# Depthwise conv of a Conformer layer: VectorE's taps merged into one instruction each, eight instead of nine taps on TensorE, and a new split of the last channel tile

## The reference, cut to what matters

```python
def conformer_conv(x, w_pw1, b_pw1, w_dw, b_dw, g_n, b_n, w_pw2, b_pw2):
    h = x @ w_pw1 + b_pw1
    a, gate = jnp.split(h, 2, axis=-1)
    h = a * jax.nn.sigmoid(gate)
    h = depthwise_conv(h, w_dw, b_dw)          # 31 taps, each channel by itself
    h = jax.nn.silu(layer_norm(h, g_n, b_n))
    return h @ w_pw2 + b_pw2
```

## Time and profile before

| | us |
|---|---|
| median of 3 runs | 3003.24 |
| lowest, highest | 3001.82, 3005.05 |
| the profiled execution's own time | 3003.5 |
| its span, first to last instruction | 3001.1 |
| TensorE busy in the span | 2876.8 |
| VectorE busy | 1640.7 |
| GpSimd busy | 911.8 |
| ScalarE busy | 749.3 |

### The profile page before, as it was taken

How to read it: one execution, slowest core, us unless ns; L and a number is a source line. 1 busy time by engine, 2 the same in 40 slices (tenths; PEclk the granted TensorE clock), 3 DMA queues, 4 the chain that set the end, 5 groups by cost and what they waited for, 6 DMA issues and landing times.

```text
span 3001.1 us, 36000 instructions
## 1 busy us (share of the span) xinstructions
PE 2876.8 (96%) x14070; PEld 2347.4 (78%) x14070; DVE 1640.7 (55%) x2612; ACT 749.3 (25%) x1717; POOL 911.8 (30%) x798
## 2 busy tenths in 40 slices
PE   8999959999999999999899899899999999999995
PEld 7888848788888888888788544487888888888884
DVE  3699974744444444444730599727444444444457
ACT  3212343221111111222111466502222111111131
POOL 3354502232233233232132333323223223223323
PEclk9999979999999999999999899999999999999998
DMA  4000003111111111111221000021111111111111
GB/s 131 29 18 25 28 1 119 29 43 31 40 43 39 33 43 43 36 43 36 71 78 32 22 1 1 23 94 36 43 36 40 31 43 43 36 36 43 43 36 70
DMA packets 158644, 124.65 MB, mean 42 GB/s; under 512 B 27905, under 2 KB 135801, under 8 KB 158488
## 3 DMA queue, kind: packets, MB, share of 16 engines
q1 hardware_dynamic: 149640, 96.83, 11.3%
q10 hardware_dynamic: 8848, 25.69, 2.3%
HBM read 112.01 MB, written 10.49 MB: 41 GB/s over the span
## 4 chain that ended last, share of the span: by engine, by line
PE 86%; DVE 9%; ACT 3%; issue 1%; DMA 0%; POOL 0%; POOLq 0%; ACTq 0%; SPq 0%; DVEq 0%
PE bank L588 26%; PE bank L593 26%; PE bank L591 26%; PE bank L953 3%; PE bank L929 2%; DVE conv_acc L1293 2%; PE bank L944 1%; DVE stats L1223 1%; DVE y L1241 1%; DVE x_lo L1249 1%; ACT y L1094 1%; DVE y L1236 1%; DVE y L1451 1%; PE bank L618 1%; ACT probs L1187 1%
## 5 line engine op out<-in xcount | busy, mean ns | idle before, releaser
L588 PE MATMUL bank<-x_hi,w_hi 128*128 128x512 f32 (+1 forms) x2688 | 957.2, 356 | 3.8 <-DVE x_lo L1249 1.6
L591 PE MATMUL bank<-x_lo,w_hi 128*128 128x512 f32 (+1 forms) x2688 | 953.4, 355 | 0.0
L593 PE MATMUL bank<-x_hi,w_lo 128*128 128x512 f32 (+1 forms) x2688 | 953.3, 355 | 0.0
L514 POOL CAST w_hi<-raw_pieces 128x512 fp32r<-128x512 f32 x348 | 329.9, 948 | 1802.9 <-issue 1363.8
L588 PEld LDWEIGHTS bank<-x_hi,w_hi 128*128 128x128 f32 x2688 | 509.5, 190 | 79.0 <-POOL w_lo L518 6.3
L591 PEld LDWEIGHTS bank<-x_lo,w_hi 128*128 128x128 f32 x2688 | 509.5, 190 | 70.6
L593 PEld LDWEIGHTS bank<-x_hi,w_lo 128*128 128x128 f32 x2688 | 509.1, 189 | 70.8
L518 POOL TENSOR_TENSOR w_lo<-raw_pieces,w_hi 128x512 fp32r<-128x512 f32 x348 | 472.2, 1357 | 27.9
L1451 DVE TENSOR_TENSOR y<-y,bank 128x512 f32<-128x512 f32 x440 | 296.2, 684 | 200.5 <-PE bank L593 198.5
L1412 DVE SCALAR_TENSOR_TENSOR gate_conv<-bank,ffn_conv_table,gate_conv 128x510 f32<-128x510 f32 x132 | 86.2, 653 | 373.5 <-ACT up_conv L1125 371.5
L1293 DVE SCALAR_TENSOR_TENSOR conv_acc<-glu,conv_table,conv_acc 128x1024 f32<-128x1024 f32 (+1 forms) x310 | 257.6, 906 | 35.4 <-ACT conv_acc L1034 35.4
(11 more groups left out here) (144 smaller groups left out, 3765.5 us busy)
## 6 DMA issues: line engine op xcount, KB each, us to landing
raw_pieces<-in_ffn_w_up_dram SPq DMA_DIRECT2D x168, 256.0 KB, 2.9
raw_pieces<-in_ffn_w_down_dram SPq DMA_DIRECT2D x84, 256.0 KB, 2.6
raw_pieces<-in_conv_w_pw_dram SPq DMA_DIRECT2D x48, 256.0 KB, 2.7
y<-in_x_prompt_dram ACTq DMA_DIRECT2D x16, 512.0 KB, 6.8
residual_dram<-y ACTq DMA_DIRECT2D x10, 512.0 KB, 2.6
y<-residual_dram ACTq DMA_DIRECT2D x10, 512.0 KB, 10.7
out_dram<-y SPq DMA_DIRECT2D x10, 512.0 KB, 2.6
raw_pieces<-in_attn_w_q_dram SPq DMA_DIRECT2D x32, 128.0 KB, 2.4
```

The source lines that it names most:

```text
L514: pool.tensor_copy(WH[:, p % RING, :], raw[:, p % RAW, :]).then_inc(piece_hi, 1)
L588: mm = pe.matmul(out, left[0], right[0], start=first, stop=False)
L591: pe.matmul(out, left[0], right[1], start=False, stop=False)
L593: return pe.matmul(out, left[1], right[0], start=False, stop=last)
```

## The change

1. `PE_TAPS` goes from 9 to 8, so VectorE has 23 taps for tiles 0 to 6 instead of 22.
2. Of these, all but the last are one instruction each, over both sequences and the 15 columns between them (1295 columns). Each waits for the one before it. The last tap stays a pair.
3. For tile 7 TensorE has 26 taps instead of 22 (`MORE_TAPS` 18), VectorE 5 instead of 9. Its sums stay in three banks (7, 6, 5). ScalarE's copies of them are gone. VectorE makes its five taps apart (`last_channels`: a tensor_scalar and four chained taps, on columns of the first chunk, then on the others), and adds each chunk's bank to them, into `conv`. `last_done` counts the three additions. TensorE's and ScalarE's work on row tiles waits for `last_done` where it waited for `conv_done`.
4. Tile 7 needs 26 high and 26 low diagonals. 24 pairs are made where 22 were; the last two pairs are made behind the high part of `glu` and ahead of two of ScalarE's copies for tile 6.
5. The row tiles of `conv_normed` are stored in another order (`NORMED_AT`), since that buffer overlays `glu` and `conv_acc`.

```diff
-    PE_TAPS = 9
-    MORE_TAPS = 13
+    PE_TAPS = 8
+    MORE_TAPS = 18
...
+                    out = bank[LAST_BANK[ch] if more else 6 + u % 2]
+                    if more and ch == 2:
+                        pe.wait_ge(sig_ready, i * 6 + 6)
+                    elif not first or u >= 2:
                         pe.wait_ge(acc_ready, i * 6 + u - 1)
...
-            pe.wait_ge(conv_done, KT)
+            pe.wait_ge(last_done, 1)
             for t in range(2):
                 turn_conv(t, KT - 1).then_inc(ct_turned, 1)
             for t in range(2, TT):
                 pe.wait_ge(ct_kept, t - 1)
+                pe.wait_ge(last_done, sum(t >= e for e in TILES_TO) + 1)
...
                         act.activation(last_glu[0], glu[:, c, :], ACT.Copy).then_inc(glu_hi_ready, 1)
+                        last_diagonals(EARLY_DIAGS, LAST_TAPS).then_inc(diag_ready, 1)
                         keep_taps(0, i, first, 1, 3)
-                        keep_taps(1, i, first)
...
-                for k in range(taps):
-                    last = k == taps - 1
-                    for c0, n, a0 in ((0, S0, 0), (S0, S1, S0 + PAD)):
-                        if k > 0:
-                            dve.wait_ge(vec_step, vs.now() - (0 if last and c0 else 1))
-                        ins = dve.scalar_tensor_tensor(
-                            out=conv[:, bass.ds(i * 2 + c, 1), c0:c0 + n] if last else acc[:, c, a0:a0 + n],
-                            in0=glu[:, c, a0 + k:a0 + k + n], scalar=tap(k), in1=acc[:, c, a0:a0 + n],
-                            op0=ALU.mult, op1=ALU.add)
-                        if not last:
-                            ins.then_inc(vec_step, vs.one())
+                n = S0 + PAD + S1
+                for k in range(taps - 1):
+                    if k > 0:
+                        dve.wait_ge(vec_step, vs.now())
+                    dve.scalar_tensor_tensor(out=acc[:, c, :], in0=glu[:, c, k:k + n], scalar=tap(k),
+                                             in1=acc[:, c, :], op0=ALU.mult, op1=ALU.add
+                                             ).then_inc(vec_step, vs.one())
                     if k == 3:
                         between()
+                dve.wait_ge(vec_step, vs.now())
+                k = taps - 1
+                for c0, n, a0 in ((0, S0, 0), (S0, S1, S0 + PAD)):
+                    ins = dve.scalar_tensor_tensor(
+                        out=conv[:, bass.ds(i * 2 + c, 1), c0:c0 + n], in0=glu[:, c, a0 + k:a0 + k + n],
+                        scalar=tap(k), in1=acc[:, c, a0:a0 + n], op0=ALU.mult, op1=ALU.add)
                 ins.then_inc(conv_done, 1)
...
-            conv_taps(1, KT // 2 - 1, taps=V_TAPS - MORE_TAPS)
+            def last_channels(a0, n, chunks):
+                tap = lambda k: conv_tab[:, KT - 1, k:k + 1]
+                part = acc[:, 1, a0:a0 + n]
+                dve.tensor_scalar(part, glu[:, 1, a0:a0 + n], tap(0), chan[:, 0, KT - 1:KT], ALU.mult, ALU.add
+                                  ).then_inc(vec_step, vs.one())
+                for k in range(1, V_TAPS - MORE_TAPS):
+                    dve.wait_ge(vec_step, vs.now())
+                    dve.scalar_tensor_tensor(out=part, in0=glu[:, 1, a0 + k:a0 + k + n], scalar=tap(k), in1=part,
+                                             op0=ALU.mult, op1=ALU.add).then_inc(vec_step, vs.one())
+                dve.wait_ge(vec_step, vs.now())
+                for ch in chunks:
+                    c0, m = CHUNKS[ch]
+                    at = GLU_COL[ch] - PAD
+                    dve.wait_ge(taps_done, 3 * (KT - 1) + ch + 1)
+                    dve.tensor_tensor(conv[:, KT - 1, c0:c0 + m], acc[:, 1, at:at + m], bank[LAST_BANK[ch]][:, 0:m],
+                                      ALU.add).then_inc(last_done, 1)
+            dve.wait_ge(conv_done, KT - 2)
+            last_channels(0, HALF, [0])
+            last_channels(HALF, HALF + PAD + S1, [1, 2])
```

More of the change, by code:

```diff
@@ L222, in trunk @@
         conv_done = sem("conv_done")
+        last_done = sem("last_channels_chunk_done")
         ct_turned = sem("conv_tile_turned")
@@ L434, in trunk @@
         EARLY = 4
+        NORMED_AT = [0, 3, 4, 5, 1, 2, 6, 7, 8, 9]
         LAST_TAPS = MORE_TAPS + PE_TAPS
@@ L439, in last_diag @@
         def last_diag(j):
-            where = slice(None), j // TILES_TO[0], cols(j % TILES_TO[0])
+            if j < EARLY_DIAGS:
+                where = slice(None), j // TILES_TO[0], cols(j % TILES_TO[0])
+            else:
+                where = slice(None), j - EARLY_DIAGS, cols(TILES_TO[0])
             return XH[where], XL[where]
         LAST_ROW = KT - 2
-        assert (LAST_TAPS - 1) // TILES_TO[0] < LAST_ROW
+        EARLY_DIAGS = LAST_ROW * TILES_TO[0]
+        LAST_BANK = [7, 6, 5]
+        assert LAST_TAPS - EARLY_DIAGS <= LAST_ROW
         last_glu = [part[:].rearrange("p k t -> p (k t)")[:, LAST_ROW * XW:LAST_ROW * XW + WIDE] for part in (XH, XL)]
@@ L654, in back_tile @@
                 for k in range(KT):
-                    mm = pe.transpose(bank[4 + 2 * (t % 2) + k // 4][:, cols(k % 4)], normed[:, t, cols(k)],
+                    mm = pe.transpose(bank[4 + 2 * (t % 2) + k // 4][:, cols(k % 4)], normed[:, NORMED_AT[t], cols(k)],
                                       ident[:])
@@ L675, in conv_taps @@
                     u = 3 * c + ch
-                    if not first or u >= 2:
+                    out = bank[LAST_BANK[ch] if more else 6 + u % 2]
+                    if more and ch == 2:
+                        pe.wait_ge(sig_ready, i * 6 + 6)
+                    elif not first or u >= 2:
                         pe.wait_ge(acc_ready, i * 6 + u - 1)
@@ L680, in conv_taps @@
                         left = last_diag(more + j) if more else (diag[:, 0, j, :], diag[:, 1, j, :])
-                        mm = product(bank[6 + u % 2][:, 0:n], left, (hi[:, at:at + n], lo[:, at:at + n]),
+                        mm = product(out[:, 0:n], left, (hi[:, at:at + n], lo[:, at:at + n]),
                                      j == -more, j == PE_TAPS - 1)
@@ L1035, in keep_taps, with last_diagonals @@
                                    bias=chan[:, 0, bass.ds(i * 2 + c, 1)]).then_inc(acc_ready, 1)
-            def last_diagonals():
+            def last_diagonals(j0, j1):
                 tables = last_hi[:].bitcast(F32), last_lo[:]
                 for part, table in enumerate(tables):
-                    for j in range(LAST_TAPS):
+                    for j in range(j0, j1):
                         ins = act.activation(last_diag(j)[part], ident[:], ACT.Copy, scale=table[:, j:j + 1])
-                ins.then_inc(diag_ready, 1)
+                return ins
             def pw1_round(i, first, last=False):
@@ L1055, in pw1_round @@
                         if last and s == 3:
-                            last_diagonals()
+                            last_diagonals(0, EARLY_DIAGS)
                     if last and c == 1:
@@ L1079, in _ @@
                 act.wait_ge(ct_turned, t + 1)
+                if t == TILES_TO[0]:
+                    act.wait_ge(last_done, 3)
                 for half in range(2):
-                    ins = act.activation(normed[:, t, half * HALF:(half + 1) * HALF],
+                    ins = act.activation(normed[:, NORMED_AT[t], half * HALF:(half + 1) * HALF],
                                          bank[2 * (t % 2) + half][:], ACT.Copy)
@@ L1325, in conv_round @@
                         conv_taps(1, i - 1, lambda: glu_low(0, i))
-            vs.rounds(dve, KT // 2 - 1, conv_round, 2 * 2 * (V_TAPS - 1))
+            vs.rounds(dve, KT // 2 - 1, conv_round, 2 * (V_TAPS - 1))
             conv_round(KT // 2 - 1, False, last=True)
-            conv_taps(1, KT // 2 - 1, taps=V_TAPS - MORE_TAPS)
+            def last_channels(a0, n, chunks):
[17 more added lines that the diff above has]
+            last_channels(HALF, HALF + PAD + S1, [1, 2])
             def conv_stats(t):
@@ L1334, in conv_stats @@
                 for half in range(2):
-                    dve.bn_stats(stats[:, t % 2, half, :], normed[:, t, half * HALF:(half + 1) * HALF]
+                    dve.bn_stats(stats[:, t % 2, half, :], normed[:, NORMED_AT[t], half * HALF:(half + 1) * HALF]
                                  ).then_inc(vec_step, vs.one())
@@ L1352, in conv_norm @@
             def conv_norm(t):
-                dve.tensor_scalar(normed[:, t, :], normed[:, t, :], mv[:, t, 0:1], rstd[:, t:t + 1],
+                dve.tensor_scalar(normed[:, NORMED_AT[t], :], normed[:, NORMED_AT[t], :], mv[:, t, 0:1], rstd[:, t:t + 1],
                                   ALU.subtract, ALU.mult).then_inc(cn_ready, 1)
```

## The result

The kernel after takes 3011.87 us (median of 7 runs, 3009.66 to 3014.59), the kernel before 3003.24 (7 runs, 2999.76 to 3005.05). The ratio is 1.003, 95% interval 1.0018 to 1.0041: some 8.6 us slower, above what the measurement can tell from nothing. Forecast were 3006.6 us and a range of 2991 to 3015. "g" is again the start of the gating of tile 7.

What follows compares the result with a forecast made beforehand. TensorE was taken to set the conv stage's pace, VectorE 3 us a tile behind. Rounds +9.8, last tile -4.7 and faster statistics -1.7 made +3.4 us on the profiled 3003.5, so a median of 3006.6 us, range 2991 to 3015.

Steps and rivals of the forecast that it cites:

- The sum: Whole kernel: the rounds, the last tile and the faster statistics, 9.8 - 4.7 - 1.7 = +3.4 us.
- VectorE's tap: VectorE's conv taps: a merged tap takes 1.55 us, 1.59 from start to start, so the merger saves nothing.
- The term of 42.8 us a run of taps: VectorE's rounds: one tile's taps including GpSimd's splits, 38.0 + 4.8 us, counted six times up to tile 7's gating.
- GpSimd in the gaps: Conv tiles: waiting merged taps let GpSimd's CAST and splits in, costing VectorE 4.8 us a tile.
- The start: Start of the conv rounds: VectorE's first taps at 96.12 - 1.76 = 94.4 us.
- The rounds: Conv tiles: VectorE becomes the bound at 44.8 us a tile against TensorE's 41.7; tile 7's gating comes 9.8 us later.
- The last tile: From tile 7's gating: first statistics at g + 56.2 instead of g + 60.9, -4.7 us; statistics 0 to 6 another -1.7.
- Behind the stage: Later stages, TensorE-bound: what the conv stage gains or loses reaches the end whole.
- the semaphore costs nothing: Rival, VectorE's taps: a waiting merged tap starts 0.07 us ahead of its forerunner's end; -5.0 us, 2998.2; 10%.
- TensorE stays the bound: Rival, conv rounds: VectorE neither waits nor loses to GpSimd; -17 us, 2986; 6%.
- Each split costs its full length: Rival, conv tiles: GpSimd's splits cost VectorE 7.6 us a tile instead of 4.8; +16.8 us, 3023; 12%.
- GpSimd stays shut out: Rival, conv tiles: splits stay out of the taps, a tile takes 43.3 us; -8.5 us, 2994.7; 12%.

Runs made afterwards that it cites:

- run 3: The kernel after with VectorE's hardware loop over the middle rounds written out as straight code: 3004.21 us, ratio 1.0005 to before.
- run 4: The kernel after with GpSimd splitting one column instead of 512 of weight pieces 8 to 31: 2997.1 us, ratio 0.9983 to before.
- run 5: The kernel of run 2 with merged, chained taps on VectorE and nine taps kept on TensorE: 3004.23 us, ratio 1.0006 to before.
- run 6: The kernel of run 2 with the first instruction of each pair waiting for everything before it: 3020.56 us, ratio 1.0062 to before.
- run 1: The kernel after with VectorE's taps of tiles 0 to 6 as pairs again, eight taps on TensorE: 3001.16 us, ratio 0.9993 to before.
- run 8: The kernel of run 1 with GpSimd's splits from piece 16 on held until VectorE finished the tile before: 2998.7 us, ratio 0.9988 to before.
- run 2: The kernel before with only the new last tile (26 taps on TensorE, 5 on VectorE): 2992.96 us, ratio 0.9971 to before.

## Why the time came out above the forecast

The time is in the stated range and at the upper edge of the forecast's own, 3001 to 3012; the forecast gave about a fourth to a time beyond +6 us. The sum was +3.4; by VectorE's timelines the seventh statistics stand at +11.5 (433.70 - 422.24). That the time missed by 5 us and not by 8 is luck: what comes back behind the stage was no part of the forecast. By its own steps:

- **VectorE's tap: the step that failed.** "One that waits for its forerunner starts 0.03 behind its end ... The merged tap therefore costs 1.59 from start to start" holds in written-out code (1.60) and not in the hardware loop (1.72), where tiles 1 to 4 lie. The term of 42.8 us a run of taps was 42.9 outside and 44.3 inside: 4 x 1.5 = 6 us. Run 3 takes them away. The gaps alone are worth more, 2.4 us a run (run 4); 0.9 of it is hidden because splits cost less in the loop. The duration, forecast 1.55, was 1.57.
- **GpSimd in the gaps: right, mechanism and size.** The CAST takes 1.34 us and the splits lie in the taps. Runs 5 and 6 show that a wait for the instruction ahead lets them in at once (run 1, that they can get in without it), run 4 that this costs 4.6 us a tile (4.8), or 3.7 in the loop. "This is what decides" claimed too much, though: with eight taps on TensorE pairs pay for the splits too. Merged taps with the loop written out (run 3) are only 0.12% above pairs (run 1), with overlapping intervals. Their tiles take 44.6 us, those of the pairs 45.0 on average; only the first run of taps, up to the gating behind it, is dearer (42.9 against 38.5). Of the 0.37% that the merger costs there, 0.25 is the loop.
- **The start: 2.1 us missed, and not by the change.** First taps 96.48, forecast 94.4. The execution of after was 2.1 us late at VectorE's first gating already; from there to the first taps it is 1.7 us less than before (30.4 against 32.1), as forecast (1.76).
- **The rounds: right in kind.** VectorE is the bound, and TensorE stands about 3 us a tile. Its clock dips (0.97 over 200 to 250) cost nothing there, as assumed. g came at +18.2 instead of +9.8: 6.3 from the rounds, mostly the loop, and 2.1 from the start of this execution.
- **The last tile: right.** -4.8 (forecast -4.7) to the first statistics, -2.0 (-1.7) to the seventh. It was forecast that both engines arrive together; TensorE came 1.16 us late. It had stood 5.72 us, not 8, and the lower clock behind it cost the forecast's 2 us or a little more: its 26 taps took 48.3 us instead of 45.8.
- **Behind the stage.** The forecast had it that what the stage loses "reaches the end whole". At the row after is 12.1 us behind (494.67 against 482.60), at the end of the span 8.7. Of the 3.4 between, about 1.4 are given back where TensorE resumes at the norm behind the second pointwise product: over the 20 us behind it the granted clock was 0.87 before and 0.94 after. The rest, some 2 us in later stages, wasn't traced to a cause.

The rivals: "the semaphore costs nothing" is refuted by the starts of the taps and run 3, "TensorE stays the bound" by TensorE's gaps. "Each split costs its full length" put the time beyond +6 us by a price that was not paid (4.6 us a tile, its point of decision 5.3); the time got there by another way. "GpSimd stays shut out" fell for this kernel, and in runs 1 and 8 pairs did not reach its 43.3 us a tile either (44.4 on average even with the splits held).

The parts of the change add up: the last tile -0.29% (run 2), the merger +0.35%, the ninth tap moved to VectorE +0.24%, together the measured +0.30%. The tap saves TensorE 1.76 us a tile that it then spends waiting. With pairs it takes VectorE's idle time, in which GpSimd did its splits; this last is read from the timelines of runs 1 and 2 and wasn't tested apart.

## What to carry to other kernels

Fewer instructions are not less time: two overlapping instructions of 1024 and 256 columns took 1.59 us, one of 1295 that waits took 1.60 or, in a hardware loop, 1.72. Look at what another engine does in the gaps that a dependence opens, and cost a wait inside a loop from a row inside that loop. A change with two halves is tried by halves: here one half alone beats both kernels.

## What the runs showed of the hardware

- A VectorE instruction that waits for the one ahead started 0.04 us behind its end in written-out code and 0.15 us behind in a hardware loop; one that waits for the one two ahead started 0.07 ahead of it.
- GpSimd's CAST, with SBUF operands, took 10 to 19 us while VectorE's tap instructions overlapped, and 0.61 to 1.66 us, for the first of a tile, while each tap waited for the one ahead. The Trainium skill, "SBUF — State Buffer", section "Who interferes with whom", gives the shared port to the first for one whole instruction. Run 1's 18.75 us span some 24 tap instructions (an estimate, from two per 1.59 us); the rule alone doesn't say why none of the ends between them let the CAST in. The CAST of 13.42 us also got in with the taps still overlapping; what let it in was not found.
- Split instructions took longer when they alternated with merged taps (2.43 for a subtraction, 1.89 for a CAST, 4.3 together) than with waiting pairs (1.35 and 1.60, or 2.15 and 0.81: 3.0 together).
- The hardware loop cost nothing where each instruction waited for the one two ahead (27.15 us for 34 instructions in it, 27.16 outside).
- TensorE ran at the lower of its two levels (1.2 GHz, matmuls of 512 columns 0.63 us apiece) for about 5 us after standing 5.72 us and for about 3 us after standing 3.72 (run 5), and was at the full level (0.40) at the second matmul after standing 1.21 us.
